# Prompt attention over units of one query block and both heads of a pair

## The reference

```python
def forgetting_attention(q, k_all, v_all, logf_all, past_len):
    ...
    ck = jnp.moveaxis(jnp.cumsum(logf_all.astype(jnp.float32), axis=1), 2, 1)
    ...
    def block(args):
        qi, cqi, bi = args
        s = jnp.einsum('bqhd,bkhd->bhqk', qi, k_all).astype(jnp.float32) * scale
        s = s + cqi[..., :, None] - ck[:, :, None, :]
        qpos = past_len + bi * qb + jnp.arange(qb)
        s = jnp.where(kpos[None, :] <= qpos[:, None], s, -jnp.inf)
        p = jax.nn.softmax(s, axis=-1)
        return jnp.einsum('bhqk,bkhd->bqhd', p.astype(v_all.dtype), v_all)
```

## Time and profile before

| | us |
|---|---|
| median of 3 runs | 1878.66 |
| lowest and highest | 1874.86, 1881.68 |
| the profiled execution | 1881.33 |
| its span | 1879.7 |

### The profile page before, as it was taken

The page is one execution under the profiler, slowest core; times in us unless marked ns, Lnnn a source line. Parts: engine busy times, 40 slices in busy tenths (PEclk is TensorE's granted clock), DMA queues, the critical chain, the costliest instruction groups (busy, mean ns, idle before and its releaser), DMA issues. The chain is left out here.

```text
span 1879.7 us, 33105 instructions
## 1 busy us (share of the span) xinstructions
PE 1723.4 (92%) x13814; PEld 1564.4 (83%) x13814; DVE 833.3 (44%) x1397; ACT 413.6 (22%) x690; POOL 176.5 (9%) x202
## 2 busy tenths in 40 slices
PE   5999999666899799899989989999999999999996
PEld 5899999554788666576638789999999999999995
DVE  5327851653788512444425633244234234334326
ACT  4210000422122100334325531111111111111112
POOL 3000000431655100000000010000000000000003
PEclk9999999655899956899989989999999999999998
DMA  6011110201222031510033211201211111111112
GB/s 179 23 54 46 45 45 11 87 2 35 79 74 78 19 84 18 151 52 0 0 124 123 90 40 51 68 23 50 63 34 46 56 34 46 57 34 50 52 75 106
DMA packets 113648, 108.40 MB, mean 58 GB/s; under 512 B 16294, under 2 KB 103807, under 8 KB 113509
## 3 DMA queue, kind: packets, MB, share of 16 engines
q1 hardware_dynamic: 110453, 105.56, 18.1%
q0 software_dynamic: 3072, 1.07, 0.5%
HBM read 93.98 MB, written 12.93 MB: 57 GB/s over the span
## 5 line engine op out<-in xcount | busy, mean ns | idle before, releaser
L2281 DVE TENSOR_TENSOR ff_acc<-ff_acc,mf_ps 128x344 f32<-128x344 f32 x264 | 135.2, 512 | 187.5 <-PE mf_ps L2424 187.3
L2417 PE MATMUL mf_ps<-h_lo,ff_w_hi 128*128 128x344 f32 x1008 | 213.8, 320 | 0.0
L2417 PE MATMUL mf_ps<-h_hi,ff_w_hi 128*128 128x344 f32 x1008 | 213.6, 320 | 0.0
L2417 PE MATMUL mf_ps<-h_hi,ff_w_lo 128*128 128x344 f32 x1008 | 212.7, 319 | 0.0
L2424 PE MATMUL mf_ps<-ff_h_hi,ff_d_hi 128*128 128x344 f32 x528 | 170.3, 322 | 3.7 <-DVE ff_h_lo L2276 3.7
L2424 PE MATMUL mf_ps<-ff_h_hi,ff_d_lo 128*128 128x344 f32 x528 | 169.9, 322 | 0.0
L2417 PEld LDWEIGHTS mf_ps<-h_hi,ff_w_lo 128*128 128x128 f32 x1008 | 169.2, 188 | 0.0
L2424 PE MATMUL mf_ps<-ff_h_lo,ff_d_hi 128*128 128x344 f32 x528 | 169.2, 320 | 0.0
L2417 PEld LDWEIGHTS mf_ps<-h_hi,ff_w_hi 128*128 128x128 f32 x1008 | 169.1, 188 | 0.0
L2417 PEld LDWEIGHTS mf_ps<-h_lo,ff_w_hi 128*128 128x128 f32 x1008 | 168.8, 188 | 0.0
L433 PE MATMUL in_ps<-h_hi,in_whi 128*128 128x344 f32 x528 | 112.8, 322 | 4.2 <-DVE in_wlo L389 4.2
(11 more groups left out here) (431 smaller groups left out, 2760.1 us busy)
## 6 DMA issues: line engine op xcount, KB each, us to landing
fs_keys<-in_cache_k_dram SPq DMA_DIRECT2D x64, 192.0 KB, 2.4
fs_values<-in_cache_v_dram SPq DMA_DIRECT2D x64, 192.0 KB, 2.5
in_raw<-in_w_in_dram SPq DMA_DIRECT2D x22, 512.0 KB, 3.8
ff_raw<-in_w_gate_dram SPq DMA_DIRECT2D x22, 512.0 KB, 3.8
ff_raw<-in_w_up_dram SPq DMA_DIRECT2D x22, 512.0 KB, 3.9
ff_d_raw<-in_w_down_dram SPq DMA_DIRECT2D x22, 512.0 KB, 5.4
ld_x<-in_x_prompt_dram SPq DMA_DIRECT2D x8, 512.0 KB, 7.2
mo_o_raw<-in_w_out_dram SPq DMA_DIRECT2D x8, 512.0 KB, 5.6
```

Of the source, the lines that this page charges most:

```text
L2281: dve.tensor_tensor(part, part, ps[:, b, 0:TG], ALU.add).then_inc(down_added, 1)
L2417: last = pe.matmul(bank(t % 2 * 3 + g)[:, 0:TG], a[:, k], b[:, k, group(g)], start=(k == 0 and n == 0), stop=(k == KD - 1 and n == 2))
```

## The change

`fox_prompt` is rewritten, without a loop, over 24 units (j, i): a pair j, a query block i, and both heads at once.

- `scores` alternates the two heads chunk by chunk. It reads q and k straight from `proj`, head 0 on partitions 0 to 63 and head 1 on 64 to 127, and writes four PSUM banks, two for each head. There is one set of these banks, where there were two buffers.
- Transposes, bias spreads, sample products and their turns go through a ring of two banks in one order (`ring`, `fill`, `empty`). DVE empties the even entries and ACT the odd ones. The bias of the next pair is spread in four pieces within the units with i of 4 to 1, into a second set of bias buffers.
- `values` takes the token values as the stationary operand (64 columns, head 0 in the lower half of the output's partitions and head 1 in the upper) and the weights as 128 moving columns. The output has channels on partitions. 1 / sum is spread over partitions by two more matmuls a unit; ACT copies the spread and DVE multiplies into `yT`.
- The bf16 matmuls, the transposes of the output, the copies of q and k and POOL's copy are gone. The causal masks are added by POOL.
- The late samples are multiplied as four at once (the first at unit 12) and two at once (unit 18), each sequence at a multiple of 32 output partitions. SP loads the last two after the first product.

The core of the diff:

```diff
-O_VALUES = [O_PROJ, O_TAIL_KV] + [O_PROJ + n * KV_BYTES for n in range(NS - 3)] + [O_TAIL_KV]
+O_VALUES = [O_PROJ, O_TAIL_KV] + [O_PROJ + n * KV_BYTES for n in (0, 1, 2, 3, 0, 1)]
...
-        q = put("q", [P, SEQ])
-        k = put("k", [P, SEQ])
...
+        bias = [[put(f"bias{s}_{e}", [P, SEQ]) for e in range(2)] for s in range(2)]
+        x = [[put(f"x{s}_{e}", [P, SEQ]) for e in range(2)] for s in range(2)]
+        units = [(j, i) for j in range(PAIRS) for i in reversed(range(NC))]
+        U = len(units)
+        neg_max = put("neg_max", [P, U, 2])
+        total = put("total", [P, U, 2])
+        spread_sb = [put(f"spread{s}", [P, P]) for s in range(2)]
+        rows = put("rows", [P, DW])
...
+        pt = [nc.alloc_sbuf_tensor_at(f"fx_pt{s}", [P, 2 * NC, P], F32, offset=O_PROJ + 4 * KV_BYTES + s * 2 * NC * P * 4)
+              for s in range(2)]
...
+        ps = ctx.enter_context(nc.psum_tensor("fx_ps", [P, 8, 512], F32))
+        scores_of = lambda e: ps[:, 2 * e:2 * e + 2].rearrange("p b n -> p (b n)")
+        ring_bank = lambda n: ps[:, 4 + n % 2]
+        out_of = lambda u: ps[:, 6 + u % 2, 0:P]
+        spread_of = lambda u: ps[:, 7 - u % 2, P:2 * P]
...
+        sample_groups = (range(EARLY, EARLY + 4), range(EARLY + 4, NS))
+        ring, of_step = [], []
+        def add(step, kind, *what):
+            of_step[step].append(len(ring))
+            ring.append((kind,) + what)
+        first_bias = []
+        for e in range(2):
+            for h in range(2):
+                first_bias.append(len(ring))
+                ring.append(("bias", 0, e, h))
...
+        for u, (j, i) in enumerate(units):
+            of_step.append([])
+            blocks = 2 * (i + 1)
+            for b0 in range(0, blocks, 4):
+                add(u, "turn", u, b0, min(b0 + 4, blocks))
+            last_turn.append(len(ring) - 1)
+            if j + 1 < PAIRS and 1 <= i <= 4:
+                bias_in[j + 1].append(len(ring))
+                add(u, "bias", j + 1, (4 - i) // 2, (4 - i) % 2)
+            if u in (12, 18):
+                s = (12, 18).index(u)
+                sample_in[s] = len(ring)
+                add(u, "values", s)
+            if u in (14, 20):
+                add(u, "rows", (14, 20).index(u))
...
+                sp.wait_ge(turned, sample_in[0] + 1)
+                for b in sample_groups[1]:
+                    load_pages(sp, m, m.cache_v, b, m.fs_values[b], m.values_in[EARLY + 1])
...
-                pool.wait_ge(neg_c_done, 1)
-                with pool.Fori(0, PAIRS) as j:
-                    pool.wait_ge(pair_done_1, j + 1)
-                    pool.tensor_copy(neg_c2[:], neg_c[:, bass.ds(j * 2, 2)]).then_inc(bias_staged, 1)
...
+                for u, (j, i) in enumerate(units):
+                    if i == NC - 1:
+                        for n in bias_in[j]:
+                            wait_copied(pool, n)
+                    for e in range(2):
+                        if i < NC - 1:
+                            pool.wait_ge(maxed, 2 * (u - 1) + e + 1)
+                        diag = bias[j % 2][e][:, i * P:(i + 1) * P]
+                        pool.tensor_tensor(diag, diag, m.causal[:], ALU.add).then_inc(masked, 1)
...
-                def scores(j, u):
-                    e, i = units[u]
-                    if u >= 2:
...
+                def scores(u):
+                    j, i = units[u]
+                    if u >= 1:
+                        pe.wait_ge(maxed, 2 * u)
                     n = (i + 1) * P
                     for b in range(0, n, 512):
                         w = min(512, n - b)
-                        last = pe.matmul(ps_s[u % 2][:, b:b + w], q[half(e), i * P:(i + 1) * P], k[half(e), b:b + w],
-                                         start=True, stop=True)
-                    last.then_inc(s_done, 1)
-                def turns(j, u):
-                    n = of_unit[u][0]
...
-                    for _ in range(2):
-                        pe.matmul(ps_t[n % 2][:, 0:2 * P], idle[:, 0:P], idle[:], start=True, stop=True)
-                    pe.wait_ge(exp_done, j * U + (u + 1))
-                    for n in of_unit[u]:
-                        _, b0, b1 = groups[n]
-                        pe.wait_ge((copied_dve, copied_act)[n % 2], j * (G // 2) + (n // 2 + 1))
-                        for b in range(b0, b1):
-                            last = pe.transpose(ps_t[n % 2][:, (b - b0) * P:(b - b0 + 1) * P],
-                                                x[u % 2][:, b * P:(b + 1) * P], m.ident[:])
-                        last.then_inc(turned, 1)
...
+                        for e in range(2):
+                            mm = pe.matmul(scores_of(e)[:, b:b + w], m.proj[half(e), T_QC + j, i * P:(i + 1) * P],
+                                           m.proj[half(e), T_KC + j, b:b + w], start=True, stop=True)
+                            if b + w == n:
+                                mm.then_inc(s_done, 1)
+                def fill(n):
+                    kind, what = ring[n][0], ring[n][1:]
+                    if n >= 2:
+                        wait_copied(pe, n - 2)
+                    bank = ring_bank(n)
+                    if kind == "bias":
+                        j, e, h = what
+                        pe.wait_ge(neg_c_done, 1)
+                        for b in range(4):
+                            last = pe.matmul(bank[:, b * P:(b + 1) * P],
+                                             neg_c[:, 2 * j + e, 4 * h + b:4 * h + b + 1].to_broadcast([P, P]), m.ident[:],
+                                             start=True, stop=True)
+                    elif kind == "turn":
+                        u, b0, b1 = what
+                        blocks = units[u][1] + 1
+                        pe.wait_ge(exp_done, 2 * u + (b1 - 1) // blocks + 1)
+                        for c in range(b0, b1):
+                            e, b = divmod(c, blocks)
+                            last = pe.transpose(bank[:, (c - b0) * P:(c - b0 + 1) * P], x[u % 2][e][:, b * P:(b + 1) * P],
+                                                m.ident[:])
+                    elif kind == "values":
+                        s, = what
+                        pe.wait_ge(m.values_in[EARLY + s], 16 * NPAGE * len(sample_groups[s]))
+                        for g in range(NPAGE):
+                            for c, b in enumerate(sample_groups[s]):
+                                last = pe.matmul(bank[c * 32:c * 32 + H, 0:DW], m.fs_p[:, b, g], m.fs_values[b][:, g],
+                                                 start=(g == 0), stop=(g == NPAGE - 1), skip_group_check=True)
...
+                    last.then_inc(turned, 1)
...
+                def values(u):
+                    j, i = units[u]
+                    pe.wait_ge(inv_done, u + 1)
+                    if u >= 1:
+                        pe.wait_ge(y_done, u)
+                    for e in range(2):
+                        spread = pe.matmul(spread_of(u)[half(e)], total[:, u, e:e + 1].to_broadcast([P, HD]), m.ident[:],
+                                           start=True, stop=True)
+                    spread.then_inc(spread_done, 1)
+                    for n in range(max(0, last_turn[u] - 1), last_turn[u] + 1):
+                        wait_copied(pe, n)
                     for b in range(i + 1):
-
-                        last = pe.matmul(ps_o[e][:, i], pt[u % 2][:, b],
-                                         m.vtok[:, b, bass.ds(j * P + e * HD, HD)], start=(b == 0), stop=(b == i))
+                        for e in range(2):
+                            last = pe.matmul(out_of(u)[half(e)], m.vtok[:, b, j * P + e * HD:j * P + (e + 1) * HD],
+                                             pt[u % 2][:, e * (i + 1) + b], start=(b == 0), stop=(b == i),
+                                             skip_group_check=True)
...
+                def shift(u, e):
+                    j, i = units[u]
+                    dve.wait_ge(s_done, 2 * u + e + 1)
+                    dve.wait_ge(masked, 2 * u + e + 1)
+                    if u >= 2:
+                        dve.wait_ge(turned, last_turn[u - 2] + 1)
+                    w = (i + 1) * P
+                    dve.tensor_tensor_reduce(x[u % 2][e][:, 0:w], scores_of(e)[:, 0:w], bias[j % 2][e][:, 0:w], -SCALE, 3e38,
+                                             ALU.add, ALU.min, neg_max[:, u, e:e + 1]).then_inc(maxed, 1)
+                def invert(u):
+                    dve.wait_ge(exp_done, 2 * u + 2)
+                    dve.reciprocal(total[:, u], total[:, u]).then_inc(inv_done, 1)
+                def finish(u):
+                    j, i = units[u]
+                    dve.wait_ge(pv_done, u + 1)
+                    dve.wait_ge(spread_copied, u + 1)
+                    dve.tensor_tensor(m.yT[:, 5 + j, i * P:(i + 1) * P], out_of(u), spread_sb[u % 2][:], ALU.mult).then_inc(
+                        y_done, 1)
...
+                for u in range(U):
```

(17 more changed lines are left out.)

261 lines of the change are left out of this document (108 added, 153 removed).

## The result

The changed kernel takes 1805.97 us (median of four runs, 1803.64 to 1807.49) where the kernel before takes 1878.7 us: 0.9605 of it, 95% interval 0.9592 to 0.9619. It is 73 us faster. The prediction was 1813 us, range 1792 to 1850, faster with 0.95.

A forecast was written before the change was run, and what follows sets the result against it. PE's own passes were taken to bound the prompt attention stage. Head 10.7, pairs 2 x 40.6 + 34.4, samples 16.5 and end 1.7 gave 144.5 us in place of 212.2, so 1813 us, range 1792 to 1850.

The forecast's parts named there:

- scores: Prompt attention, per pair of heads: score passes overlap two at a time, 10.5 us where before they took 15.4.
- transposes: Transposes of the weights in prompt attention: 72 x 0.108 = 7.7 us a pair, the same before and after.
- bias in the loop: Bias passes on PE, in four pieces between units: 32 x 0.117 = 3.8 us a pair, none in the third.
- late samples with turns: Late sample products on PE, two passes at a time: 15.4 us, 16.5 with turns and changes, where before 31.
- waits in the loop: PE waiting for shifts and copies within units: 5.2 us a pair with bias, 2.8 in the third.
- Overlap of parts that differ in rows or columns alone: PE passes in scores and values: assumed to overlap two at a time, though the rows shown differ in both.
- Rival (b): Handoffs bind: PE waits for DVE and ACT twice as long as summed, 13 us more, 1827 us; chance 0.12.
- Masks on POOL: Causal masks moved to POOL, 0.28 to 0.83 us each, hidden by other heads' work; uncovered 13 us.
- (c): PE's clock drops for a quarter of the prompt attention stage: 24 us more, 1837 us; chance 0.13.
- (d): Slower than before: PE's clock at 0.50 through the whole prompt attention stage, +95 us, 1908 us; chance 0.04.
- Rival (e): Better than the sum: four sample groups overlap fully (5 less), ring waits don't show (13 less), 1795 us; chance 0.09.
- the booked gain: Removing two idle bf16 matmuls per unit ahead of PE's transposes: 0.22 x 16 = 3.5 us saved per pair.

## Why the prediction was right, and where its terms were off

PE's own time of the stage, from each group's start to the next with waits apart, beside the sum (a shape change of 1.2 a pair is put to each of scores, values and transposes):

| term, us | predicted | after |
|---|---|---|
| head, without its scores, with 2.8 of waits | 10.7 | 11.2 |
| scores | 31.5 + 3.6 = 35.1 | 28.2 |
| values and spreads | 29.4 + 3.6 = 33.0 | 32.8 |
| transposes | 23.1 + 3.6 = 26.7 | 30.5 |
| bias in the loop | 7.6 | 8.5 |
| late samples with turns | 16.5 | 11.5 |
| waits in the loop | 13.2 | 12.2 |
| end | 1.7 | 1.2 |
| stage | 144.5 | 136.1 |

- **What bounds it**, and that only PE's passes had to be counted, was right. The sum was taken from the profiled execution of before (1881.33 us); from the median it would have been 1811. DVE and ACT, taken as near 80 us, were busy for 70.7 and 64.1. Outside the stage the span is 1666.7 us, before 1667.5.
- **Overlap of parts that differ in rows or columns alone** was taken from rows that differ in both. It is right: without the rows' overlap the stage takes an estimated 18 us more (three times the 6.0 of a pair), and 7 more by the clock at its head; without most of the columns' overlap it takes 14.3 more.
- **The scores were mis-sized**, 35.1 for 28.2. The step that failed is that the first and the last pass of four stand alone, which took the passes to start in the written order. With one slot of 0.213 per block for the pair, i + 1 slots and 0.21 for the change of shape, the trace's 1.71, 1.49, 1.28 and 1.06 for i = 6 to 3 come out within 0.01.
- **The samples were mis-sized**, 16.5 for 11.5. The step that failed is "both passes of a matmul are in one group and start in order, so I take two at a time". Four do overlap: the trace gives 20.8/5.3 = 3.9. The samples one after the other show why: a pass of another group starts ahead of up to four waiting ones, so the passes don't have to start in order. That is also what the scores' sum had wrong. The 3.9 is the "up to 4x" of the Trainium skill, "TensorEngine Tiling (Array Packing)", section Theoretical Speedup. The Trainium skill's "TensorE: Matmul & The Clock Gate", section Measured speedup vs the span model, has 2.38x for three column tiles, by an estimate from that figure a fifth below the ideal; in this trace, with 16 rounds in a row, no such loss is seen.
- **The transposes were mis-sized** the other way, 26.7 for 30.5. The pitch of 0.108 was right, but a group that PE waits behind ends with its own latency: eight take 1.09 us of PE, 0.136 each. The same holds for the bias pieces, 7.6 for 8.5: the sum priced a pass at 0.117, the row of a value pass, and eight took 1.09.
- **Waits** came to 12.2 for 13.2. For i = 7 to 5 they were 0.8, 0.6 and 0.5, not 0.8 each, and those at the pair's end 1.3, not 1.5. Rival (b) did not occur.
- **Masks on POOL** are hidden, as said: 48 x 0.455 = 21.7 us of POOL that nobody waits for.
- **The clock** held, as (c) and (d) were judged unlikely. The kernel without idle matmuls shows that (d) was a real danger of this stage, and I had judged it by the clock before, which came with those matmuls. The right outcome there was partly luck: I can't say from a row why the new order holds its clock.
- **Rival (e)** came true in one half: the samples' full overlap, but not the ring without waits.

## What to carry to other kernels

When a contraction or an output uses half or a quarter of the array, give the parts in turn to neighbouring passes: rows and columns overlapped fully here, but only passes within about four of each other. Before you take out matmuls that compute nothing, run the kernel without them alone and look at the granted clock: the booked gain was 10 us and the measured loss 67 to 100. Put work that is ready ahead of work that waits for another engine's copy.

## What the runs showed of the hardware

- Passes on disjoint parts of the array start before earlier ones on another part have started: four of them at a seam of two runs of 16. With runs of four passes the order no longer mattered.
- Samples in four groups of 32 columns run at 3.9 times the rate of one (64 passes in 5.3 us for 20.8), in two groups at 1.95 times (32 in 5.33 for 10.4). Value passes on two halves of the columns stand 0.058 us apart, one by one 0.107.
- The clock fell to 0.50 behind the wait at the head in several kernels: for some 3 us in the kernels with scores head by head, samples one after the other and masks on DVE, for 6 us with the first scores ahead of the sums, for 17 us in the three with both heads from the same rows, and in the old kernel without idle matmuls for 82 to 85 us in each pass of the loop. In the one profile of the changed kernel it did not fall. At 0.50 PE was busy for all of the 15 us shown with the same rows, and for 244.7 of 252 us in the old kernel. What separates them stays open; with the samples one after the other it can't be the code, which is the changed kernel's up to there.
